# Three pairs of gate and up chunks of the second feed forward computed as seven block products, with VectorE making four weight differences for each

## The reference

```python
D_FF_2 = ((8 * D_MODEL + 767) // 768) * 256          # 2816
h2 = rmsnorm(x, norm_ffn[layer])
x = x + (jax.nn.silu(h2 @ w_gate[layer]) * (h2 @ w_up[layer])) @ w_down[layer]
return rmsnorm(x, norm_final)
```

## Time and profile before

| | |
|---|---|
| median of 3 runs | 726.73 us (726.69 to 726.86) |
| profiled execution | 726.56 us |
| its span | 724.7 us |
| PE busy | 715.0 us (99%) |
| DVE busy | 516.7 us (71%) |
| ACT busy | 410.6 us (57%) |
| mean granted TensorE clock | 0.998 |

### The profile page before, as it was taken

One profiled execution on the slowest core, in us unless ns is written; L12 is line 12 of the kernel. 1 busy time (PEld: TensorE's weight loads), 2 busy tenths in 40 slices (PEclk: granted clock), 3 DMA queues, 4 the chain that ended last, 5 costly groups with the idle time before them and its releaser, 6 DMA issues.

```text
span 724.7 us, 9660 instructions
## 1 busy us (share of the span) xinstructions
PE 715.0 (99%) x3746; PEld 572.5 (79%) x3746; DVE 516.7 (71%) x911; ACT 410.6 (57%) x691; POOL 25.9 (4%) x43
## 2 busy tenths in 40 slices
PE   8999999999999999999999999999999999999996
...
GB/s 363 415 370 229 387 104 356 204 59 261 225 180 230 203 264 242 224 175 115 162 202 291 117 119 148 151 165 121 115 229 232 178 196 202 179 175 175 175 58 59
DMA packets 72989, 145.94 MB, mean 201 GB/s; under 512 B 4128, under 2 KB 27680, under 8 KB 71920
## 3 DMA queue, kind: packets, MB, share of 16 engines
...
q10 hardware_dynamic: 288, 0.27, 0.1%
...
## 4 chain that ended last, share of the span: by engine, by line
PE 95%; issue 2%; DVE 1%; ACT 1%; POOL 0%; POOLq 0%; DVEq 0%
PE bank L441 23%; PE bank L443 23%; PE bank L442 23%; PE bank L786 5%; PE bank L423 5%; PE bank L784 3%; PE bank L460 1%; PE bank L515 1%; PE bank L523 1%; PE bank L518 1%; PE bank L918 1%; PE bank L940 1%; PE bank L624 1%; PE bank L500 1%; PE bank L646 1%
## 5 line engine op out<-in xcount | busy, mean ns | idle before, releaser
L1579 DVE TENSOR_TENSOR WL<-W,WH 128x1024 fp32r<-128x1024 f32 (+2 forms) x222 | 249.7, 1169 | 35.4 <-ACT WH L1071 35.3
L1071 ACT ACTIVATE WH<-W 128x1024 fp32r<-128x1024 f32 (+2 forms) x222 | 211.9, 1011 | 49.7 <-DMA W<-in_w_mlp 35.8
L441 PE MATMUL bank<-WH,AHL 128*128 128x512 f32 (+1 forms) x480 | 188.8, 393 | 0.0
L443 PE MATMUL bank<-WH,AHL 128*128 128x512 f32 (+1 forms) x480 | 185.3, 386 | 0.0
L442 PE MATMUL bank<-WL,AHL 128*128 128x512 f32 (+1 forms) x480 | 185.2, 386 | 0.0
L441 PEld LDWEIGHTS bank<-WH,AHL 128*128 128x128 f32 x480 | 90.2, 188 | 20.4 <-issue 3.2
L443 PEld LDWEIGHTS bank<-WH,AHL 128*128 128x128 f32 x480 | 90.2, 188 | 18.7
L442 PEld LDWEIGHTS bank<-WL,AHL 128*128 128x128 f32 x480 | 90.3, 188 | 17.0
L441 PE MATMUL bank<-WH,HH 128*128 128x512 f32 (+1 forms) x218 | 84.9, 390 | 0.0
L443 PE MATMUL bank<-WH,HL 128*128 128x512 f32 (+1 forms) x218 | 84.5, 388 | 0.0
L442 PE MATMUL bank<-WL,HH 128*128 128x512 f32 (+1 forms) x218 | 84.4, 387 | 0.0
...
## 6 DMA issues: line engine op xcount, KB each, us to landing
W<-in_w_mlp SPq DMA_DIRECT2D x32, 1024.0 KB, 5.4
W<-in_w_in SPq DMA_DIRECT2D x24, 1024.0 KB, 5.0
...
W<-in_w_down SPq DMA_DIRECT2D x11, 1024.0 KB, 4.9
W<-in_w_ada SPq DMA_DIRECT2D x10, 1024.0 KB, 8.6
WX<-in_w_ada SPq DMA_DIRECT2D x10, 1024.0 KB, 10.4
W<-in_w_out SPq DMA_DIRECT2D x8, 1024.0 KB, 5.3
```

Source lines behind the costliest of these rows:

```text
L441: e.matmul(po, hs, wh[:, k, c0:c0 + cw], start=first and k == 0, stop=False)
L443: ins = e.matmul(po, ls, wh[:, k, c0:c0 + cw], start=False, stop=last and k == unit.nk - 1)
L1071: e.activation(m.WH[unit.slot][:, c], m.W32[unit.slot][:, c], ACT.Copy).then_inc(S["w_hi"], 1)
L1579: e.tensor_tensor(m.WL[unit.slot][:, c], m.W32[unit.slot][:, c], m.WH[unit.slot][:, c].bitcast(F32), ALU.subtract).then_inc(S["w_lo"], 1)
```

## The change

**Seven products in place of eight.** Three pairs of neighbouring chunks, (3,4), (5,6) and (7,8), are each taken together; the other five chunks stay as they are. With 512 columns of gate and 512 of up a pair is a product of 2x2 blocks. On the left stand the activations A: rows are the two token blocks, columns the two halves of the inner dimension. On the right stand the weights B: B11 and B21 are the two halves of `w_gate`, B12 and B22 those of `w_up`. Eight block products become seven, by sums on both sides that are chained (each uses the one before):

- activations, made once: s1 = A21 + A22, s2 = s1 - A11, s4 = A12 - s2, s3 = A11 - A21 (`FS`, with halves `FH` and `FL`);
- weights, made for each pair: t1 = B12 - B11, t2 = B22 - t1, t4 = B21 - t2, t3 = B22 - B12 (`make(g, 0)` to `make(g, 3)`), each in two DVE instructions of 128x1024 on the loaded floats;
- products: A11 B11 (bank 4), s1 t1 (bank 5), s2 t2 (bank 6), and then onto what the bank holds s4 B22 (bank 5), s3 t3 (bank 6), A12 B21 (bank 4), A22 t4 (bank 6);
- between them ACT copies bank 4 to `quad_g1`, and DVE adds in five steps of 128x512: `u1` and `u0` (in the place of `g1b`) take up, `quad_g1` takes the gate of the second token block.

A pair needs seven units with both halves (B11, t1, t2, B22, t3, B21, t4) where its two chunks had four. Five of them are loaded (t3 starts as B12, and t4 as a second load of B21), t1 and t2 are written into slots without a load. The ring gets a seventh slot. The `w_down` part is unchanged but for its grouping. A pair's `hid` is 512 wide, so its turn has four transposes for a token block. Bank 6 is in use in a pair, so both turns of a pair go to bank 7 (`turns["n"] = 1`), and the second waits until DVE has read the first.

The list of work is now in groups (g): 0, 1, 2, then the pairs 3, 4, 5, then 6 and 7 (chunks 9 and 10). PE starts the first two products of the next group (`begin(g + 1)`) ahead of a pair's turns. Renamed semaphores, which the diff also has, are left out here, as is the last squares' scratch tile.

```diff
         self.hT = self.S2[:, :].rearrange("p (k t) -> p k t", k=8)
+        self.W32.append(M("W32_6", 76, [128, 2048]))
+        self.WL.append(M("WL_6", 76, [128, 2048], F32R))
+        self.WH.append(M("WH_6", 8, [128, 2048], F32R))
+        self.FH = [M(f"FH{i}", 60 + 2 * i, [128, 4, 128], F32R) for i in range(4)]
+        self.FS = [M(f"FS{i}", 68 + 2 * i, [128, 4, 128]) for i in range(4)]
+        self.FL = [M(f"FL{i}", 68 + 2 * i, [128, 4, 128], F32R) for i in range(4)]
+        self.g1 = M("quad_g1", 6, [128, 512])
+        self.junk = M("junk", 60, [128, 1024])
+        self.u0, self.u1 = self.g1b[:, 0:512], self.g1b[:, 512:1024]
         self.bank = [ctx.enter_context(nc.psum_tensor(f"bank{i}", [128, 512], F32)) for i in range(8)]
         self.turn_bank = {}
...
+PAIRS = (3,5,7)
+GROUPS = [(c, c in PAIRS) for c in range(11) if c - 1 not in PAIRS]
+NG = len(GROUPS)
...
+    def quad_unit(g, n, src, i):
+        c0 = 256 * GROUPS[g][0]
+        add(("gu", g), src, 4 * i, 4, [(src, c0, 512)], True, ("gu_mm", QUAD_AT[g] + n + 1))
+        return units[-1]
+
+    def made_unit(g, n):
+        unit = Unit(4, 512, [], True, (S["gu_mm"], QUAD_AT[g] + n + 1))
+        unit.made = True
+        units.append(unit)
+        by["gu", g].append(unit)
+        return unit
...
+            b11 = quad_unit(g, 0, "w_gate_2", 0)
+            t1 = made_unit(g, 1)
+            at = len(units)
+            down_units(g - 1)
+            down = units[at:]
+            t2 = made_unit(g, 2)
+            b22 = quad_unit(g, 3, "w_up_2", 1)
+            t3 = quad_unit(g, 4, "w_up_2", 0)
+            b21 = quad_unit(g, 5, "w_gate_2", 1)
+            t4 = quad_unit(g, 6, "w_gate_2", 1)
+            loads += [b11, t3, t1, b22, t2, *down, t4, b21]
...
+        slot = 6 if unit.made and 6 not in holds else min(holds, key=holds.get)
...
+        t1, t2, _, t3, _, t4 = by["gu", g][1:]
+        t3.base, t4.base = t3.landed, t4.landed
+        t1.landed, t2.landed, t4.landed, t3.landed = ((S["made"], 8 * n + 2 * i + 2) for i in range(4))
...
+    def hid_turn2(g, tb):
+        if GROUPS[g][1]:
+            turns["n"] = 1
+        hid_turn(g, 4 if GROUPS[g][1] else 2, tb, ("hid2", HID_AT[g, tb], 16 + 2 * g + tb + 1))
...
+    def quad_sum(g, n, i, bk, first):
+        part(by["gu", g][n], m.FH[i], m.FL[i], 0, 0, bk, first, True, "gu_mm", lambda k: ("kx", 9 + i), onto=not first)
+
+    def begin(g):
+        if GROUPS[g][1]:
+            part(by["gu", g][0], m.AH, m.AL, 0, 0, 4, True, True, "gu_mm", n_ready(2, 0))
+            quad_sum(g, 1, 0, 5, True)
+        else:
+            up2(g, 0)
+
+    def rest(g):
+        if not GROUPS[g][1]:
+            up2(g, 1)
+            for tb in range(2):
+                down2(g - 1, tb, g == 1, False)
+            return
+        q = quads.index(g)
+        down2(g - 1, 0, False, False)
+        quad_sum(g, 2, 1, 6, True)
+        down2(g - 1, 1, False, False)
+        w.wait_ge(S["quad"], 5 * q + 1)
+        quad_sum(g, 3, 2, 5, False)
+        frees(5, ("quad", 5 * q + 3))
+        w.wait_ge(S["quad"], 5 * q + 2)
+        quad_sum(g, 4, 3, 6, False)
+        w.wait_ge(S["quad_act"], q + 1)
+        part(by["gu", g][5], m.AH, m.AL, 4, 0, 4, False, True, "gu_mm", n_ready(2, 0), onto=True)
+        frees(4, ("silu", SILU_AT[g, 0]))
+        w.wait_ge(S["quad"], 5 * q + 4)
+        part(by["gu", g][6], m.AH, m.AL, 4, 1, 6, False, True, "gu_mm", n_ready(2, 1), onto=True)
+        frees(6, ("quad", 5 * q + 5))
...
+    for g in range(2, NG - 1):
+        rest(g)
+        if GROUPS[g][1]:
+            begin(g + 1)
+            hid_turn2(g, 0)
+            hid_turn2(g, 1)
+        else:
+            hid_turn2(g, 0)
+            hid_turn2(g, 1)
+            if g < NG - 2:
+                begin(g + 1)
...
+    def quad_group(g):
+        q = quads.index(g)
+        w.wait_ge(S["gu_mm"], QUAD_AT[g] + 1)
+        if q:
+            w.wait_ge(S["quad"], 5 * q)
+        copy(m.g1[:, :], bank[4][:, :], "quad_act")
+        hi(5)
+        hi()
+        w.wait_ge(S["gu_mm"], QUAD_AT[g] + 6)
+        w.wait_ge(S["hid2"], HID_AT[g - 1, 0])
+        e.activation(m.rel[0][:, :], bank[4][:, :], ACT.Silu).then_inc(S["silu"], 1)
+        hi()
+        w.wait_ge(S["quad"], 5 * q + 5)
+        w.wait_ge(S["hid2"], HID_AT[g - 1, 1])
+        e.activation(m.rel[1][:, :], m.g1[:, :], ACT.Silu).then_inc(S["silu"], 1)
+        hi(2)
...
+    def form(i):
+        a11, a12, a21, a22 = (m.hT[:, k:k + 4, t:t + 128] for t in (0, 128) for k in (0, 4))
+        s1, s2, s4, s3 = (f[:, :, :] for f in m.FS)
+        if i == 0:
+            tt(s1, a21, a22, ALU.add, "x_adds")
+        elif i == 1:
+            w.wait_ge(S["x_adds"], 5)
+            tt(s2, s1, a11, ALU.subtract, "x_adds")
+        elif i == 2:
+            w.wait_ge(S["x_adds"], 6)
+            tt(s4, a12, s2, ALU.subtract, "x_adds")
+        else:
+            tt(s3, a11, a21, ALU.subtract, "x_adds")
+
+    def form_lo(i):
+        w.wait_ge(S["mx_act"], 9 + i)
+        tt(m.FL[i][:, :, :], m.FS[i][:, :, :], m.FH[i][:, :, :].bitcast(F32), ALU.subtract, "kx")
+
+    def make(g, n):
+        b11, t1, t2, b22, t3, b21, t4 = by["gu", g]
+        base, a, b = ((t1, t3, b11), (t2, b22, t1), (t4, t4, t2), (t3, b22, t3))[n]
+        if base.made:
+            for old in base.old:
+                w.wait_ge(old.free[0], old.free[1])
+        if n == 0:
+            w.wait_ge(b11.landed[0], b11.landed[1])
+            w.wait_ge(t3.base[0], t3.base[1])
+        elif n == 1:
+            w.wait_ge(b22.landed[0], b22.landed[1])
+            w.wait_ge(t1.landed[0], t1.landed[1])
+        elif n == 2:
+            w.wait_ge(t4.base[0], t4.base[1])
+            w.wait_ge(t2.landed[0], t2.landed[1])
+        for p in range(2):
+            c = slice(1024 * p, 1024 * p + 1024)
+            tt(m.W32[base.slot][:, c], m.W32[a.slot][:, c], m.W32[b.slot][:, c], ALU.subtract, "made")
+
+    def quad_group(g):
+        q = quads.index(g)
+        following = GROUPS[g + 1][1]
+        lo(1 + GROUPS[g - 1][1])
+        make(g, 2)
+        lo()
+        w.wait_ge(S["gu_mm"], QUAD_AT[g] + 2)
+        w.wait_ge(S["quad_act"], q + 1)
+        if q:
+            w.wait_ge(S["hid2"], HID_AT[quads[q - 1], 1])
+        tt(m.u1, bank[5][:, :], m.g1[:, :], ALU.add, "quad")
+        make(g, 3)
+        lo()
+        w.wait_ge(S["gu_mm"], QUAD_AT[g] + 3)
+        tt(m.u0, bank[6][:, :], m.g1[:, :], ALU.add, "quad")
+        lo(3)
+        w.wait_ge(S["gu_mm"], QUAD_AT[g] + 4)
+        w.wait_ge(S["quad"], 5 * q + 2)
+        tt(m.u0, bank[5][:, :], m.u0, ALU.add, "quad")
+        w.wait_ge(S["gu_mm"], QUAD_AT[g] + 5)
+        tt(m.u1, bank[6][:, :], m.u1, ALU.add, "quad")
+        if following:
+            make(g + 1, 0)
+        lo()
+        w.wait_ge(S["gu_mm"], QUAD_AT[g] + 7)
+        tt(m.g1[:, :], bank[6][:, :], m.g1[:, :], ALU.add, "quad")
+        if following:
+            make(g + 1, 1)
+        lo()
+        w.wait_ge(S["hid_turned"], 4 + 2 * (g - 2) + 2)
+        w.wait_ge(S["silu"], SILU_AT[g, 0])
+        w.wait_ge(S["quad"], 5 * q + 4)
+        tt(m.hid[g % 2][:, 0, :], m.u0, m.rel[0][:, :], ALU.mult, "hid2")
+        w.wait_ge(S["silu"], SILU_AT[g, 1])
+        tt(m.hid[g % 2][:, 1, :], m.u1, m.rel[1][:, :], ALU.mult, "hid2")
+        lo(0 if following else 2)
...
+        else:
+            following = GROUPS[g + 1][1]
+            if following:
+                make(g + 1, 0)
+            lo()
+            gated(g, 0)
+            if following:
+                make(g + 1, 1)
+            lo()
+            gated(g, 1)
+            lo(0 if following else 1)
```

More of the change, by code:

```diff
@@ L187, in __init__ @@
         self.nk, self.wid, self.pieces, self.split, self.free = nk, wid, pieces, split, free
+        self.made = False
     def block(self, m):
@@ new lines, in quad_unit @@
+    def quad_unit(g, n, src, i):
[8 more added lines that the diff above has]
+        return unit
+    loads = list(units)
+    for g in range(NG + 1):
+        if g < NG and GROUPS[g][1]:
+            b11 = quad_unit(g, 0, "w_gate_2", 0)
[9 more added lines that the diff above has]
+            loads += [b11, t3, t1, b22, t2, *down, t4, b21]
+            continue
+        at = len(units)
+        if g < NG:
+            c = GROUPS[g][0]
+            for i in range(2):
+                add(("gu", g), "w_gate_2", 4 * i, 4, [("w_gate_2", 256 * c, 256), ("w_up_2", 256 * c, 256)],
+                    True, ("gu_mm", GU_AT[g, 1] - 1 + i))
+        if g:
+            down_units(g - 1)
+        loads += units[at:]
@@ L278, in weight_units @@
+    gate_up = loads.index(by["gu", 0][0])
     slots = [2, 4, 12, 5, 3, 0, 13, 1, 2, 4, 12, 5, 3, 0, 13, 1, 2, 3, 4, 5, 0, 1]
     slots += [2, 12, 3, 13, 4, 14, 5, 15, 0, 1, 2, 12, 3, 13, 4, 5]
-    while len(slots) < len(units):
+    while len(slots) < gate_up:
         slots.append((2, 3, 0, 1, 4, 5)[(len(slots) - 38) % 6])
+    used = []
+    for g in range(NG):
+        if GROUPS[g][1]:
```

(32 more changed lines are left out.)

218 lines of the change are left out of this document (116 added, 102 removed).

## The result

The changed kernel takes 745.93 us (median of 4 runs, 744.71 to 748.39), the kernel before beside it 726.8. The ratio is 1.0267, with a 95% interval of 1.0241 to 1.0294: 19 us slower. The forecast was 740.0, in a band of its own of 736 to 743.5, with 746 as the rival in which the clock falls as well. The profiled run took 746.28 us.

What follows compares the result with a forecast made beforehand. PE was taken to bound the kernel, with DVE becoming slower inside pairs. 726.56 - 8.16 + 4.3 + 5.8 + 1.7 + 5.8 + 3.9 = 739.9, forecast as 740.0 us; band 736 to 743.5, wider range 732 to 748.

Steps and rivals of the forecast that it cites:

- A: Stall from the first pair's start to the second pair's t1: DVE's backlog makes PE wait 4.3 us.
- B: Stall at each exit between pairs: one-bank turn idles PE 4.4 us; with slow low halves after it, 5.8.
- B's steps: After an exit's turn, `w_down`'s other three low halves come every 1.137 us, PE needs 0.68: 1.4 us.
- A2: Stall in the second pair: DVE is done 30.3 us after `w_down` starts, PE needs 28.6; PE waits 1.7.
- C: Stall at the third pair's exit into a plain chunk: the second turn waits 3.9 us for HL.
- The 36 matmuls: Three pairs: seven parts of gate and up instead of eight save 36 matmuls, 8.16 us, all on PE's path.
- DVE's price for `make`: Weight differences in pairs: each 128x1024 instruction takes DVE 1.137 us, the same as a low half.
- the 5 us of cover: Loads: each has over 5 us between landing and use, so they were entered at nothing.
- the clock rival: Half-speed products after pauses at three exits: 8.2 us, less 1.7 taken back, giving 746; chance 0.17.
- The prediction's own sign: Changed profile: granted clock stays at 1.00 in all stretches, or the rival with a falling clock holds.
- only the turn costs: Rival: faster DVE, `make` at its lower bound, shrinks A to 0.6, removes A2: 734.6 us; chance 0.12.
- it is faster because DVE was half idle: Rival: DVE's idle half covers everything, the whole 8.16 us saving stays: 718.6 us; chance 0.05.

Runs made afterwards that it cites:

- e4: Changed kernel with each pair's second turn in bank 6 and, on DVE, `w_down`'s low halves made ahead of both HL: 735.19 us, ratio 1.0115.
- e3: Changed kernel with 64 matmuls that nobody reads, filling PE's waits at t1, between turns and at the last exit: 741.42 us, ratio 1.0201.
- e10: Changed kernel with only `w_down`'s low halves made ahead of both HL, both turns still in bank 7: 742.12 us, ratio 1.0222.
- e1: Changed kernel with only chunks 5 and 6 taken as a pair, the other nine chunks plain: 730.89 us, ratio 1.0059.
- e2: Changed kernel with the weight differences of `make` replaced by DVE copies of the first operand (results wrong): 739.86 us, ratio 1.0174.
- e7: Changed kernel with pairs (3,4) and (7,8) only, both edits of e4, and two DVE sums moved ahead of low halves: 723.0 us, ratio 0.9945.
- e8: As e7, but pairs (3,4) and (6,7), with one plain chunk between them: 726.13 us, ratio 0.9992 against the kernel before.
- e9: Changed kernel with only each pair's second turn moved to bank 6, low halves of `w_down` still behind HL: 736.26 us, ratio 1.0136.
- e6: Changed kernel with pairs (3,4) and (7,8) only, two plain chunks between, the change's own exits: 736.08 us, ratio 1.0127.

## Why the prediction was right, and where it was short

The mechanism was as forecast; one term stood at nothing and was not nothing. PE's starts in the changed kernel, shown above, give each stall. PE's own time is taken as in the prediction: 2.72 us a product, 1.36 a part with `w_down`, 0.7 for two turns.

| from, to (us) | length | PE's own | late | forecast |
|---|---|---|---|---|
| 578.65 (turn of chunk 2), 610.98 (t1) | 32.33 | 27.54 | 4.8 | A 4.3 |
| 610.98, 620.83 (`w_down`) | 9.85 | 3.42 | 6.4 | B 4.4 |
| 620.83, 651.73 (next t1) | 30.90 | 27.20 | 3.7 | B's steps 1.4, A2 1.7 |
| 651.73, 659.97 (`w_down`) | 8.24 | 3.42 | 4.8 | B 4.4 |
| 659.97, 692.88 (last exit) | 32.91 | 29.92 | 3.0 | B's steps 1.4 |
| 692.88, 697.08 | 4.20 | 0.35 | 3.9 | C 3.9 |
| 697.08, 715.36 (turn of chunk 9) | 18.28 | 16.67 | 1.6 | 0 |
| sum | | | 28.2 | 21.5 |

(578.65 is a turn like the ones shown; the kernel before has it at 578.16, and its turn of chunk 9 would be at 578.16 + 7 x 16.80 = 695.8.) The sum closes: 28.2 - 8.16, less 7 x 0.13 = 0.9 by which the prediction's own time for a chunk is short of 16.80, gives 19.1, and with the start's 0.49 it is 19.6, the difference of the two spans (744.3 - 724.7). The 28.2 are more than the 17.1 us of waits, since PE's matmuls also took 8.0 us longer at half clock. The other 3.1 are small terms: the 0.9 just named, and an estimated 1.8 for eleven waits, because a matmul's record lasts 0.39 us where its step is 0.23, and the view counts idle time only from the record's end.

**What was right.** The 36 matmuls. DVE's price for `make`, 1.13 us a step. DVE's run without a gap through the first pair. A, in place and nearly in size: half a microsecond more, since HL came at 581.06, where 580.0 was forecast, half of it the later start and half a load of `w_down`, issued at 573.40. ACT's high copies begin only when it is there, 5.35 us later and not 4.9:

```profile
578.75 2.01 ACT L1192 ACTIVATE WH<-W 128x1024 fp32r<-128x1024 f32 x2 [4.96 <-DMA W<-in_w_down]
```

A2, in place. The two exits, with their waits at HL and at WL: the second is 0.4 over, the chain of the turn being 5.39 us and not 5.1. C is exact. No wait of PE for a load, and none of more than 0.2 us for anything that was not named. Not each load has the 5 us of cover that the prediction gives it, though: in e4 DVE waits 0.43 us for one of `w_gate`.

**What was mis-sized: the clock, entered at nothing.** The step that failed is the weight given to the clock rival, 0.17, on the ground that no row shows a fall inside the work. The prediction's own sign says so too: the clock stays at 1.00 in all stretches, or the rival holds. The measured 745.9 lies outside the forecast's own band (736 to 743.5) and in the wider range only because that takes in the rival. The table has the clock in three places. The first product with t1 took 1.6 us longer than the second (4.46 against 2.85); the stretch from 659.97, with the clock low for the first 6 us, is 1.6 over; so is the last one. That is 4.8 us of the 6.7 by which the stalls exceed the forecast. e3, which only kept PE busy, came out 4.5 us below the changed kernel, and is shorter in the same three places, by 1.55, 1.45 and 1.44 us. The 8.0 us at half clock are not all loss to the kernel: a part of them lies where PE would have waited for DVE afterwards.

The rival foresaw the place only in part. It had one slow product behind each pause at an exit, 8.2 in all less 1.7. In the trace the first fall comes ahead of the exit, behind a pause of 2.04 us at t1 with two shorter ones ahead of it, and the longest lasts over six microseconds of full work. That it arrived at 746 is in part luck: its 6.5 on 740 is here 5 for the clock and the rest for small terms.

On the clock the Trainium skill ("TensorE: Matmul & The Clock Gate", under "HAM oscillation — how this bites in real kernels") says that pauses between bursts of matmuls bring the throttle, and the next burst starts cold. The trace agrees at four places. It also shows that this isn't a certainty at each pause: e10 has the same waits ahead of t1 as the changed kernel (2.06 and 2.04 us), and its product with t1 runs at full clock, 613.51 - 610.64 = 2.87 us. The wait of 3.60 at its last exit brings no fall either, and in the changed kernel and in e1 the same wait does.

**The other rivals.** That only the turn costs (734.6, `make` at its lower bound): e2 made it so and gave 739.9. Stall A came out as the rival has it, 28.23 - 27.54 = 0.7. The rival took 8 x 0.46 = 3.7 us off a pair, and the copies of e2, two of them in 1.20 us from start to start where two differences take 2.27, take off 8 x 0.535 = 4.3. The kernel of e2 lost 8.5 us of clock as well, so the rival's 734.6 and the clock's part together may explain its time, but the split isn't measured. That it is faster because DVE was half idle: refuted for pairs in a row. The prediction asked for two things there, a load of DVE under 30.9 us and a covered turn. e2 has the first (30.7) without the second, and is 13 us slower than the kernel before. The rival holds in part for pairs apart with a covered turn (e7). What pairs in a row lack is room for DVE. A pair asks 35.0 us of it in 30.9 of PE's, so 4.1 have to come from a plain chunk, which had 8.1 us idle before. By that sum one chunk is enough, yet it still left a wait of 2.07 us (e8); two left nearly none (e7). The sum over a stretch doesn't say when each half is due.

**What stays open.** What exactly decides whether the clock falls at a pause of 2 to 3.6 us; the runs show both. How much of the gain of e9 and e10 is shorter waits and how much is falls that didn't come. How much of e7's gain over e6 is due to each of its three edits; they were only run together. Three neighbouring pairs with the exits mended and PE kept busy were not run.
